# Turning the second block's heads on VectorE instead of TensorE

## The reference, cut to what matters

```
proj = rmsnorm(x, g_mix) @ w_in
qa, ka, va, qb, kb, vb, fl, qc, kc, vc, qi, ki, wi, gl = split(proj)
a:  z = (qa . ka) * DH**-0.5     # 8 heads of 64, stick breaking
b:  z = (qb . kb) * DH**-0.5     # 8 heads of 64, with forget gates from fl
c:  qc, kc, qi, ki are rotated (the first 16 of 64 features of each head)
    dots  = (qi . ki) * IDX_DIM**-0.5          # 4 index heads
    score = sum over heads of wi * NI**-0.5 * relu(dots), causal
    the best 64 keys of each token are kept
    z = (qc . kc) * DH**-0.5     # 8 query heads, 2 key heads
y = gated sum of the three groups' outputs, then w_out and the MLP
```

## Time and profile before

| | |
|---|---|
| median of 3 runs | 1801.98 us (1801.94 to 1802.05) |
| the profiled execution's own time | 1802.17 us |
| its span | 1800.2 us |
| PE busy | 1781.3 us, 99% of the span |
| POOL busy | 1360.4 us, 76% |
| ACT busy | 1048.1 us, 58% |
| DVE busy | 762.8 us, 42% |

### The profile page before, as it was taken

How to read it: one execution, slowest core, us unless ns; L and a number is a source line. 1 busy time by engine, 2 the same in 40 slices (tenths; PEclk the granted TensorE clock), 3 DMA queues, 4 the chain that set the end, 5 groups by cost and what they waited for, 6 DMA issues and landing times.

```text
span 1800.2 us, 25415 instructions
## 1 busy us (share of the span) xinstructions
PE 1781.3 (99%) x9235; PEld 1489.3 (83%) x9235; DVE 762.8 (42%) x1342; ACT 1048.1 (58%) x1563; POOL 1360.4 (76%) x573
## 2 busy tenths in 40 slices
PE   7999999999999999999999999999999999999998
PEld 4888888888888888888888878898888888889887
DVE  2782344843334446343337374321113765431112
ACT  4645675445677654466655666555555566746554
POOL 5867787866778877676879766778887865688886
PEclk9999999999999999999999999999999999999999
DMA  9875556754556667455647544556655644456653
GB/s 368 312 232 164 164 176 210 235 156 137 158 180 187 177 206 232 138 152 150 193 135 223 152 130 140 175 170 193 188 189 171 195 142 131 149 178 195 189 186 129
DMA packets 171554, 327.88 MB, mean 182 GB/s; under 512 B 10433, under 2 KB 16065, under 8 KB 171457
## 3 DMA queue, kind: packets, MB, share of 16 engines
q1 hardware_dynamic: 168272, 320.22, 57.4%
q10 hardware_dynamic: 3184, 6.32, 1.0%
HBM read 325.46 MB, written 1.05 MB: 181 GB/s over the span
## 4 chain that ended last, share of the span: by engine, by line
PE 69%; POOL 15%; issue 14%; DMA 1%; ACT 0%; POOLq 0%; DVE 0%; SPq 0%; DVEq 0%; ACTq 0%
PE G L1925 16%; PE G L1927 16%; PE G L1926 16%; POOL wlo L529 15%; PE A L2651 3%; PE G L2651 2%; PE A L1925 2%; PE A L1927 2%; PE A L1926 2%; PE A L2652 1%; PE G L2652 1%; PE A L2394 1%; PE G L2416 1%; DMA raw<-in_w_in 1%; PE A L1979 1%
## 5 line engine op out<-in xcount | busy, mean ns | idle before, releaser
L529 POOL TENSOR_TENSOR wlo<-raw,whi 128x1024 fp32r<-128x1024 f32 (+1 forms) x568 | 1356.7, 2399 | 426.2 <-ACT whi L554 423.7
L554 ACT ACTIVATE whi<-raw 128x1024 fp32r<-128x1024 f32 (+1 forms) x568 | 593.4, 1048 | 570.0 <-PE G L1927 432.3
L1925 PE MATMUL G<-whi,hparts 128*128 128x512 f32 (+1 forms) x1472 | 581.9, 395 | 1.0 <-DVE hparts L1301 0.6
L1927 PE MATMUL G<-whi,hparts 128*128 128x512 f32 (+1 forms) x1472 | 568.1, 386 | 0.0
L1926 PE MATMUL G<-wlo,hparts 128*128 128x512 f32 (+1 forms) x1472 | 567.8, 386 | 0.0
L1925 PEld LDWEIGHTS G<-whi,hparts 128*128 128x128 f32 x1472 | 276.4, 188 | 59.3 <-issue 5.2
L1927 PEld LDWEIGHTS G<-whi,hparts 128*128 128x128 f32 x1472 | 276.3, 188 | 56.9
L1926 PEld LDWEIGHTS G<-wlo,hparts 128*128 128x128 f32 x1472 | 276.8, 188 | 51.0
L1925 PE MATMUL G<-whi,osplit 128*128 128x512 f32 x240 | 94.2, 393 | 0.0
L1927 PE MATMUL G<-whi,osplit 128*128 128x512 f32 x240 | 93.4, 389 | 0.0
L1926 PE MATMUL G<-wlo,osplit 128*128 128x512 f32 x240 | 93.4, 389 | 0.0
(11 more groups left out here) (433 smaller groups left out, 2561.2 us busy)
## 6 DMA issues: line engine op xcount, KB each, us to landing
raw<-in_w_in SPq DMA_DIRECT2D x324, 512.0 KB, 3.8
raw<-in_w_up SPq DMA_DIRECT2D x64, 512.0 KB, 3.7
raw<-in_w_down SPq DMA_DIRECT2D x64, 512.0 KB, 3.5
raw<-in_w_out SPq DMA_DIRECT2D x40, 512.0 KB, 3.7
raw<-in_w_branch_out SPq DMA_DIRECT2D x36, 512.0 KB, 4.3
modw<-in_w_mod SPq DMA_DIRECT2D x32, 512.0 KB, 5.4
raw<-in_w_branch SPq DMA_DIRECT2D x24, 512.0 KB, 3.5
modz<-in_w_mod SPq DMA_DIRECT2D x16, 512.0 KB, 9.9
```

The source lines that it names most:

```text
L529: pool.tensor_tensor(wlo[:, s, :, 0:n], raw[:, s, :, 0:n], whi[:, s, :, 0:n].bitcast(F32), ALU.subtract)\
L554: act.activation(whi[:, slot, :, 0:n], raw[:, slot, :, 0:n], ACT.Copy).then_inc(hi_ready, 1)
L1925: pe.matmul(bank, hi, whi[:, slot, kk, 0:n], start=first, stop=False)
L1927: return pe.matmul(bank, lo, whi[:, slot, kk, 0:n], start=False, stop=last)
```

## The change

PE turns no heads any more, ACT copies none. DVE turns them from `z2` to `t2` in blocks of 32x32, for which it has an instruction of its own. One instruction takes 32 partitions (tokens) and all heads and both token tiles at once, writes 32 partitions (features), and 16 of them cover a range of columns. They are 16 each for QC, QA, KA, QB and KB (256 columns), 16 for QI and 16 for KC (128 columns) and 16 for KI (64 columns): 128 a layer. `dup` is gone, since the same rows of KC and KI are written to both halves. The factor `DH ** -0.5` goes into the evacuation of QA and QB (`rstd_q`, from `rms`), and for the third group into KC, by one instruction behind the rotation. The rotation's tables are copied from SBUF to the PSUM bank A[3], and two of its four temporaries lie there too (all banks of A and G are PSUM; `z2`, `t2`, `rt2` and `rope_2` are SBUF).

PE waits for four counts of `heads_turned` (QC, QI, KC, KI) before the index dots, and for four more (QA, KA, QB, KB) before the running sum.

```diff
+                link(dve.tensor_scalar(rstd_q[:], rms[:, 0:TT], DH ** 0.5, None, ALU.mult))
+                dve.reciprocal(rstd_q[:], rstd_q[:]).then_inc(query_scale, 1)
+                angles = A[3][:, 0:TT * 2 * ROT].rearrange("p (t c n) -> p t c n", t=TT, c=2)
+                spare = A[3][:, TT * 2 * ROT:].rearrange("p (q n) -> p q n", q=2)
+                link(dve.tensor_copy(angles, rope_2[:]))
                 dve.wait_ge(evacuated, w(evacuated, 2 * TT + 3 * TT))
...
-                        temps = [rt2[:, q, 0:nh * ROT].rearrange("p (h n) -> p h n", h=nh) for q in range(4)]
+                        temps = [(spare if q % 2 == 0 else rt2)[:, q // 2 if q % 2 == 0 else q, 0:nh * ROT].rearrange("p (h n) -> p h n", h=nh)
+                                 for q in range(4)]
...
-                for t in range(TT):
-                    for c in range(2):
-                        dve.tensor_copy(dup[:, t, 0:2, c * DH:(c + 1) * DH],
-                                        z2[:, t, KC:KC + 2 * DH].rearrange("p (g n) -> p g n", g=2))
-                        ins = dve.tensor_copy(dup[:, t, 2, c * DH:(c + 1) * DH], z2[:, t, KI:KI + DH])
-                ins.then_inc(roped, 1)
+                link(dve.tensor_scalar(z2[:, :, KC:KC + 2 * DH], z2[:, :, KC:KC + 2 * DH], DH ** -0.5, None, ALU.mult))
+
+                turn_heads(t2[:, 16:20], QC, 4, P)
+                turn_heads(t2[:, 20:22], QI, 2, P)
+                turn_heads(t2[:, 22:24], KC, 2, DH)
+                turn_heads(t2[:, 24:25], KI, 1, DH)
+                for a, col in enumerate((QA, KA)):
+                    dve.wait_ge(evacuated, w(evacuated, TT))
+                    turn_heads(t2[:, 4 * a:4 * a + 4], col, 4, P)
...
+                for a, col in enumerate((QB, KB), 2):
+                    dve.wait_ge(evacuated, w(evacuated, TT))
+                    turn_heads(t2[:, 4 * a:4 * a + 4], col, 4, P)
                 dve.wait_ge(forget_log, w(forget_log))
```

On ACT, and on PE:

```diff
-                for c, col in enumerate(SECOND):
-                    evacuate((c + 1) % 2, [z2[:, t, col:col + CH] for t in range(TT)], ACT.Copy, scale,
-                             beside=lambda s, c=c: copy_beside(c, s))
+                act.wait_ge(query_scale, w(query_scale))
+                for c, col in enumerate(SECOND):
+                    evacuate((c + 1) % 2, [z2[:, t, col:col + CH] for t in range(TT)], ACT.Copy,
+                             [rstd_q[:, t:t + 1] for t in range(TT)] if col in (QA, QB) else scale)
...
                     for s in range(SLOTS):
                         slab(G[2 * p:2 * p + 2], *h_pairs, s)
-                        turn_beside(c, s)
-                pe.wait_ge(turned_copied, w(turned_copied, 4))
+                pe.wait_ge(heads_turned, w(heads_turned, 4))
...
-                pe.wait_ge(evacuated, w(evacuated, TT))
+                pe.wait_ge(evacuated, w(evacuated, 2 * TT))
+                pe.wait_ge(heads_turned, w(heads_turned, 4))
```

More of the change, by code:

```diff
@@ L213, in build @@
         esel = sb_at("esel", [P, NF, P], BF16, cb)
-        dup = sb_at("dup", [P, TT, 3, P], F32, cb + 2048)
         work = sb_at("work", [P, 3 * P], F32, cb + 5120)
@@ L276, in build @@
         rstd_sq = sb("rstd_sq", [P, TT])
+        rstd_q = sb("rstd_q", [P, TT])
         gate2 = [sb_at(f"gate2_{n}", [P, TT, CH], F32, at) for n, at in enumerate((
@@ L363, in build @@
         sm_normed, heads_out = sem("sm_normed"), sem("heads_out")
+        query_scale, heads_turned = sem("query_scale"), sem("heads_turned")
         last_rstd, out_scaled = sem("last_rstd"), sem("out_scaled")
@@ L386, in build @@
         SECOND = [QA, KA, QB, KB, VA]
-        BESIDE = {(2, 1): (0,), (2, 2): (1,), (3, 0): (2,), (3, 1): (3,), (3, 2): (4,), (3, 3): (5,),
-                  (4, 0): (8, 9), (4, 1): (10, 11, 12), (4, 2): (6, 7)}
         MOD_ORDER = (0, 2, 1, 3)
@@ L1696, in layer @@
                 token_scale()
+                link(dve.tensor_scalar(rstd_q[:], rms[:, 0:TT], DH ** 0.5, None, ALU.mult))
[3 more added lines that the diff above has]
+                link(dve.tensor_copy(angles, rope_2[:]))
                 dve.wait_ge(evacuated, w(evacuated, 2 * TT + 3 * TT))
                 for t in range(TT):
-                    cos, sin = (rope_2[:, t, c] for c in range(2))
+                    cos, sin = (angles[:, t, c] for c in range(2))
                     for col, nh in ((QC, 10), (QI, 5)):
                         v = z2[:, t, col:col + nh * DH].rearrange("p (h n) -> p h n", n=DH)
-                        temps = [rt2[:, q, 0:nh * ROT].rearrange("p (h n) -> p h n", h=nh) for q in range(4)]
+                        temps = [(spare if q % 2 == 0 else rt2)[:, q // 2 if q % 2 == 0 else q, 0:nh * ROT].rearrange("p (h n) -> p h n", h=nh)
+                                 for q in range(4)]
                         link(rotate(v[:, :, 0:ROT], v[:, :, ROT:2 * ROT], cos.unsqueeze(1).to_broadcast([P, nh, ROT]),
                                     sin.unsqueeze(1).to_broadcast([P, nh, ROT]), temps))
-                for t in range(TT):
-                    for c in range(2):
-                        dve.tensor_copy(dup[:, t, 0:2, c * DH:(c + 1) * DH],
-                                        z2[:, t, KC:KC + 2 * DH].rearrange("p (g n) -> p g n", g=2))
-                        ins = dve.tensor_copy(dup[:, t, 2, c * DH:(c + 1) * DH], z2[:, t, KI:KI + DH])
-                ins.then_inc(roped, 1)
+                link(dve.tensor_scalar(z2[:, :, KC:KC + 2 * DH], z2[:, :, KC:KC + 2 * DH], DH ** -0.5, None, ALU.mult))
[6 more added lines that the diff above has]
+                    turn_heads(t2[:, 4 * a:4 * a + 4], col, 4, P)
                 for t in range(TT):
@@ L1724, in layer @@
                 ins.then_inc(forget_ready, 1)
-                dve.wait_ge(evacuated, w(evacuated, 5 * TT))
+                dve.wait_ge(evacuated, w(evacuated, TT))
                 link(dve.tensor_scalar(wis[:], z2[:, :, WI:WI + NI], NI ** -0.5 * DH ** -0.5, None, ALU.mult))
@@ L2457, in layer @@
                     chunk(G[2 * (n % 2):2 * (n % 2) + 2], *h_pairs, width, free=evacuated)
[L2458 to L2470, removed]
-                            pe.wait_ge(evacuated, w(evacuated, TT))
[L2472 to L2479, removed]
                 for c in range(len(SECOND)):
                     p = (c + 1) % 2
-                    if c < 4:
-                        pe.wait_ge(evacuated, w(evacuated, TT))
+                    pe.wait_ge(evacuated, w(evacuated, TT))
                     for s in range(SLOTS):
                         slab(G[2 * p:2 * p + 2], *h_pairs, s)
-                        turn_beside(c, s)
-                pe.wait_ge(turned_copied, w(turned_copied, 4))
+                pe.wait_ge(heads_turned, w(heads_turned, 4))
                 qa, ka, qb, kb, qc, qi = (t2[:, 4 * a:4 * a + 4] for a in range(6))
```

## The result

| | before | changed |
|---|---|---|
| median (6 runs each) | 1801.96 us (1801.83 to 1802.32) | 1790.17 us (1789.84 to 1791.47) |
| the profiled execution's span | 1800.2 us | 1788.2 us |

The ratio is 0.9935, with a 95% interval of 0.9924 to 0.9946: 11.8 us faster by the medians, 12.0 by the spans.

What follows compares the result with a forecast made beforehand. PE was taken as the bound, busy 99% of the span; 1802.2 - 12.0 = 1790.2 us, taken as 1790.5 for the thin reserve, with DVE's 59.4 us a layer fitting its room. The range was 1789.0 to 1802.

Steps and rivals of the forecast that it cites:

- PE's gain: Over the chunks from QA to VA, PE drops 50 transposes a layer: 5.98 us a layer, 12.0 us in all.
- DVE's sum: DVE's work from the rotation's start to the place behind the turned heads: 59.4 us against 60.3 and 60.2 of room.
- rotation: On DVE, with tables and two temporaries in PSUM: four passes, 4.5 us a layer, upper end 30 us.
- key factor: One DVE instruction from SBUF to SBUF: 0.3 to 2.7 us with its wait, taken as 1.5.
- forget gates' first part: On DVE: 0.9 us in the first layer, 4.3 more in the second, taken as 3.0.
- 128 transposes: DVE's turning of the heads in one layer: 50.4 us, 0.394 on average, with bounds of 34.7 and about 190.
- No wait for POOL: DVE's transposes would not wait for POOL; the rival that they do had chance 0.04 and gave 2068 us.
- The reserve: DVE done with less than 1 us to spare ahead of PE's running sum, so PE doesn't wait.
- DVE is late by a little: Rival, chance 0.25: PE waits 1 to 6 us a layer for DVE's transposes, 1792 to 1802, in the middle 1796.
- a part of the delay vanishes: DVE's chain behind the transposes has a wait of about 2 us for POOL, where part of the delay could vanish.
- The rival of the slower kernel: VectorE becomes this stage's bound, chance 0.17: 1842 us at half column speed (0.07), or something between, 1803 to 1815 (0.10).
- PE's gain being lost to POOL: Rival, chance 0.04: POOL or its DMA falls behind through five chunks; a third of the gain lost gives 1794.

Runs made afterwards that it cites:

- the other order: Changed kernel with the third group's 64 transposes reordered so four in a row (QC, QI, KC, KI) write the same 32 partitions: 1789.98 us.
- 0.9 us more: Changed kernel with two more 256-column transposes a layer behind those of KB, into memory nobody reads: 1795.92 us.
- 3.6 us more: Changed kernel with eight more 256-column transposes a layer behind those of KB, into memory nobody reads: 1797.13 us.
- 9.0: Changed kernel with twenty more 256-column transposes a layer behind those of KB, into memory nobody reads: 1806.63 us.

## Why the prediction was right

It gave 1790.5 us and the profiled execution took 1790.18. By its steps:

**PE's gain**, 5.98 us a layer: right. The evacuations are 10.88 apart, and the transposes put back cost 11.4 us.

**DVE's sum**, 59.4 us: 58.9 in the first layer (1012.48 - 953.54) and 58.5 in the second. Each from its first start to the next term's:

| term | predicted | first layer |
|---|---|---|
| rotation | 4.5 | 4.05 |
| key factor | 1.5 | 1.50 |
| forget gates' first part | 3.0 | 3.15 |
| 128 transposes | 50.4 | 35.81 + 14.43 = 50.24 |

The agreement of the sum is in part luck. The key factor and the forget gates' first part were taken from inside wide bounds, 0.3 to 2.7 and 0.9 to 5.2 us, and how long they take hangs on where POOL is: 1.70 and 2.49 in the second layer, 0.33 and 0.97 in the first layer of the run with the rotation in SBUF, where both met a gap of POOL. One reading was off without harm: in the rotation of before 12 of 24 instructions took about 2.4 us, not most.

A transpose of 256 columns starts 14.39 / 32 = 0.450 us after the one before; 0.452 was predicted. The two rows that it was built on, a column at about 1 ns and no overlap across groups of partitions, hold for this operation as well. The first is now measured on it: (436 - 303) / 128 = 1.04 ns a column. The second is shown by the other order: 48 of the 64 transposes no longer change their output partitions, and 6.0 us go, 0.125 each, where the prediction had 0.09. The Trainium skill ("VectorE: DVE Perf Modes", Two Vector instructions with no wait between them) says that an instruction that writes to another group of 32 partitions than the last output is held until the earlier ones are done; the runs agree, and without the hold DVE's row is shorter by what they show.

**No wait for POOL** in the transposes: right; the longest of 256 took 0.444 us. The rotation with one operand left in SBUF didn't wait either (4.05 us), with two it did (32.7). The Trainium skill ("SBUF — State Buffer", Who interferes with whom) has this as a rule, that an instruction with two SBUF inputs contends with a GpSimd instruction that reads SBUF; the trace agrees. One operand in SBUF can wait too, though: the key factor took 1.46 us here and 0.29 where it met a gap of POOL, and `wis` 2.37 with two more transposes. Why the transposes and the rotation get past POOL and these two don't, no run here shows.

**The reserve** was the step that was mis-sized. The prediction had DVE wanted after 58.8 us and 1.5 more of PE's own lead, so that PE waits for all above an average of 0.400 us a transpose, one for one. DVE needed 58.9, and the lead of PE is indeed 1.55. But it can't be used up: the place between is the gap that POOL leaves for `fgw` and `wis`, and of it 0.86 us were left by `fgw` and 0.59 by `wis`. The run with 0.9 us more is past both; nothing between was run. Past that PE's wait comes as a step of some 2 us a layer, about the same with 3.6 us more, and is 5.67 with 9.0. The rival "DVE is late by a little" priced lateness one for one; that its middle, 1796, is what 0.9 us more gave is chance. The prediction's remark that a part of the delay vanishes in the wait of the chain's last instruction held, with 1.96 us. Had the transposes of a layer been 0.9 us longer in all, 2%, the time would have been about 1796. That the kernel kept clear of this by so little, and the forecast with it, is luck: the prediction didn't know of the place. The row that tells of the gap stood in the trace of before, with POOL's next instructions 0.93 us behind the start of `fgw` at 1018.44, and the prediction didn't read it. POOL's timeline, before:

```profile
1019.37 4.81 POOL L529 TENSOR_TENSOR wlo<-raw,whi 128x1024 fp32r<-128x1024 f32 x2 [1.93 <-ACT whi L554]
```

Less the 6.0 us of PE's gain this is 1013.37, where it came (1013.34).

**The rival of the slower kernel** would have needed DVE to be later by something between 3.6 us a layer (1797) and 9.0 (1807). With the rotation in SBUF it is later by 25 us (1840). PE's gain being lost to POOL is out: in the chunks from QB on POOL itself waits for ACT twice in four slabs (0.90 and 0.32 us), and PE waits nowhere in the five chunks.

## What to carry to other kernels

Work that moves from the bounding engine to one with idle time is worth what it took from the first, as long as the other's row ends before its next consumer, so cost that row instruction by instruction and look for the first thing that misses its place, not only for the last. An instruction that needs a gap of another engine makes a step of its lateness: 0.9 us a layer cost 5.7 in the median here. An edit that is worth nothing alone, as the tables in PSUM, can be what another edit stands on; run both halves.

## What the runs showed of the hardware

- One instruction on DVE with both operands in SBUF waits for the POOL instruction under way, and the next one again for POOL's next: of the three `fgw` two took 2.40 and 2.39 us and the last 0.16 (two more transposes, first layer). A run of such instructions doesn't get through in one wait. `wis`, with one operand in SBUF, waited for 2.37 us in the second layer of that run; of 256 transposes none took more than 0.444.
- TensorE's clock fell behind a wait of 5.67 us (granted 0.50 in the 6 us that followed, matmuls of 128x256 at 1.19 us for two instead of 0.59); behind waits of 1.93 and 2.11 us it stayed at 1.00 in the profiled executions. Other runs of those two kernels had a mean of 0.997, so it isn't shown that it always does.
- In an unbroken row on the same output partitions a transpose also shows a shorter time of its own: 260 instead of 303 ns for 128 columns, 194 instead of 236 for 64, while those of 256, the first of each four, stay at 437.
